# Stick-breaking scores issued for two heads at once, one on each half of TensorE's rows

## The reference, cut to what matters

```python
def stick_breaking_attention(q, k, v):
    # A[t,s] = sigmoid(z_ts) * prod_{s<j<t} (1 - sigmoid(z_tj)), s < t;  o_t = sum_s A[t,s] v_s
    ...
    def block(args):
        q_blk, start = args
        z = jnp.einsum("bhqd,bhkd->bhqk", q_blk, kh) * scale
        q_pos = start + jnp.arange(SB_BLOCK, dtype=jnp.int32)
        mask = k_pos[None, :] < q_pos[:, None]
        log_keep = jnp.where(mask, jax.nn.log_sigmoid(-z), 0.0)
        between = lax.cumsum(log_keep, axis=3, reverse=True) - log_keep
        weight = jnp.where(mask, jnp.exp(jax.nn.log_sigmoid(z) + between), 0.0)
        return jnp.einsum("bhqk,bhkd->bhqd", weight, vh)
    ...
```

## Time and profile before

| | us |
|---|---|
| median of 3 runs | 1779.08 |
| lowest, highest | 1778.29, 1780.57 |
| the profiled execution's own time | 1775.79 |
| its span, first to last instruction | 1773.9 |
| PE busy | 1720.2 |
| DVE, ACT, POOL busy | 283.3, 197.6, 143.5 |
| mean granted TensorE clock | 0.982 |

### The profile page before, as it was taken

One profiled execution on the slowest core, in us unless ns is written; L12 is line 12 of the kernel. 1 busy time (PEld: TensorE's weight loads), 2 busy tenths in 40 slices (PEclk: granted clock), 3 DMA queues, 4 the chain that ended last, 5 costly groups with the idle time before them and its releaser, 6 DMA issues.

```text
span 1773.9 us, 41158 instructions
## 1 busy us (share of the span) xinstructions
PE 1720.2 (97%) x18812; PEld 1268.8 (72%) x18812; DVE 283.3 (16%) x553; ACT 197.6 (11%) x462; POOL 143.5 (8%) x164
## 2 busy tenths in 40 slices
PE   7999999999999995999999999999999999999997
PEld 6788577777778755777777776777776777777774
DVE  2333310000434334001001001001001001001002
ACT  3123220000322323000000000000000000000000
POOL 2233200000123322000000000000000000000000
PEclk9999999999999996999999999999999999999999
DMA  8213244443320324999999999899899899899892
GB/s 308 73 46 120 95 152 168 168 153 132 122 102 27 119 95 143 308 350 341 315 350 333 322 351 326 296 349 353 304 350 346 278 348 352 303 352 354 298 353 97
DMA packets 311445, 432.58 MB, mean 244 GB/s; under 512 B 9051, under 2 KB 263261, under 8 KB 311277
## 3 DMA queue, kind: packets, MB, share of 16 engines
q1 hardware_dynamic: 310396, 427.75, 69.9%
q0 software_dynamic: 672, 2.14, 0.4%
q10 hardware_dynamic: 208, 0.08, 0.0%
HBM read 428.90 MB, written 1.05 MB: 242 GB/s over the span
## 4 chain that ended last, share of the span: by engine, by line
PE 94%; DVE 2%; ACT 1%; issue 1%; POOL 1%; SPq 0%; DMA 0%; DVEq 0%
PE ps L848 34%; PE ps L861 23%; PE ps L751 8%; PE ps L488 7%; PE ps L762 3%; PE ps L629 3%; PE ps L497 3%; PE ps L873 2%; PE ps L600 1%; PE ps L615 1%; PE ps L826 1%; PE ps L611 1%; PE ps L621 1%; PE ps L512 1%; PE ps L519 1%
## 5 line engine op out<-in xcount | busy, mean ns | idle before, releaser
L848 PEld LDWEIGHTS ps<-bv_sb,ring 128*64 128x64 f32 x14336 | 598.1, 137 | 92.6 <-issue 92.6
L848 PE MATMUL ps<-bv_sb,ring 128*64 128x96 f32 x14336 | 619.0, 247 | 6.2 <-issue 5.6
L861 PE MATMUL ps<-ring,LT_sb 128*96 128x512 f32 x896 | 410.9, 601 | 0.0
L861 PEld LDWEIGHTS ps<-ring,LT_sb 128*96 128x96 f32 x896 | 137.0, 163 | 191.6 <-issue 179.3
L1505 DVE TENSOR_TENSOR LT_sb<-LT_sb,ps 128x192 f32<-128x192 f32 x112 | 39.7, 354 | 916.8 <-ACT LT_sb L1132 916.8
L751 PE MATMUL ps<-hT_sb,ring 128*128 128x256 f32 (+1 forms) x768 | 155.7, 362 | 0.0
L751 PEld LDWEIGHTS ps<-hT_sb,ring 128*128 128x128 f32 x768 | 136.0, 190 | 24.6 <-issue 9.1
L1132 ACT ACTIVATE LT_sb<-ps 128x192 f32<-128x192 f32 x112 | 37.0, 330 | 948.9 <-PE ps L848 948.9
L488 PE MATMUL ps<-hT_sb,ring 128*128 128x256 f32 x608 | 139.4, 388 | 0.0
L488 PEld LDWEIGHTS ps<-hT_sb,ring 128*128 128x128 f32 x608 | 117.6, 196 | 17.0 <-DVE qk_sb L1220 0.5
L1556 POOL TENSOR_SCALAR small<-small 128x1 f32<-128x1 f32 x16 | 4.1, 254 | 1346.3 <-ACT XT_sb L951 1320.5
(11 more groups left out here) (259 smaller groups left out, 1002.9 us busy)
## 6 DMA issues: line engine op xcount, KB each, us to landing
ring<-in_moe_w_gate SPq DMA_DIRECT2D x112, 1024.0 KB, 5.9
ring<-in_moe_w_up SPq DMA_DIRECT2D x112, 1024.0 KB, 8.9
ring<-in_moe_w_down SPq DMA_DIRECT2D x112, 1024.0 KB, 10.8
ring<-in_ffn_w_gate SPq DMA_DIRECT2D x11, 1024.0 KB, 5.3
ring<-in_ffn_w_up SPq DMA_DIRECT2D x11, 1024.0 KB, 7.9
ring<-in_ffn_w_down SPq DMA_DIRECT2D x11, 1024.0 KB, 9.8
ring<-in_w_in SPq DMA_DIRECT2D x14, 768.0 KB, 6.4
ring<-in_w_out SPq DMA_DIRECT2D x8, 768.0 KB, 5.5
```

Source lines behind the costliest of these rows:

```text
L848: ins = mm(o[lo:lo + P // 2, :], w[:, k, i * P + lo:i * P + lo + P // 2], xgT[:, k, :], start=(k == 0), stop=(k == KD - 1))
L861: ins = mm(bank(2 + half)[0:SLOTS, :], moe_hid[c % 2][:, i, :], d[:, i, half * 512:(half + 1) * 512], start=(c == 0 and i == 0), stop=(c = ...
```

## The change: what it does

`sb_scores` takes a pair of heads `p` in place of one head. It issues the 256-column matmul of head 2p (partitions 0 to 63), that of head 2p+1 (partitions 64 to 127), then the two 128-column matmuls. The pairs stand ahead of the loop (heads 0 and 1) and at the end of levels 1, 3 and 5; at the end of levels 0, 2, 4 and 6 there are no scores any more. Each head's signal `sbz_ps` still comes from its 128-column matmul.

The two heads of a pair are in PSUM at once: even heads keep bank 6, odd heads get bank 3 (`sb_bank`), for the scores and for the running sum. Bank 3 was used by the key products and by `X M1` of group 1. So the first scores wait until VectorE has read the key products (`LT_ready`, `AT_ready`), `X M1` goes to bank `g`, the bank of the product that it follows, and the state product in bank 3 waits until the last head is through (`sb_expo`).

```diff
+        def sb_bank(h):
+            return bank(3 if h % 2 else 6)
...
-            def sb_scores(L, h):
-
-                if h:
-                    pe.wait_ge(sb_expo, SB_H * L + h)
+            def sb_scores(L, p):
+
+                if p:
+                    pe.wait_ge(sb_expo, SB_H * L + 2 * p)
                 else:
                     pe.wait_ge(*evac_sem(L, S_Z + 1))
-                pe.wait_ge(*evac_sem(L, S_SB + 1 + 2 * (h // 2)))
-                r = (h % 2) * SB_D
-                kh, qh = sk_v[r:r + SB_D, h // 2, :], sq_v[r:r + SB_D, h // 2, :]
-                o = bank(6)
-                mm(o[:, 0:T], kh[:, 0:P], qh[:, 0:T], start=True, stop=True)
-                mm(o[:, T:T + P], kh[:, P:T], qh[:, P:T], start=True, stop=True).then_inc(sbz_ps, 1)
+                    pe.wait_ge(LT_ready, 2 * (L + 1))
+                    pe.wait_ge(AT_ready, 2 * (L + 1))
+                pe.wait_ge(*evac_sem(L, S_SB + 1 + 2 * p))
+                heads = [(sk_v[r:r + SB_D, p, :], sq_v[r:r + SB_D, p, :], sb_bank(2 * p + r // SB_D)) for r in (0, SB_D)]
+                for kh, qh, o in heads:
+                    mm(o[:, 0:T], kh[:, 0:P], qh[:, 0:T], start=True, stop=True)
+                for kh, qh, o in heads:
+                    mm(o[:, T:T + P], kh[:, P:T], qh[:, P:T], start=True, stop=True).then_inc(sbz_ps, 1)
...
-                        ins = mm(bank(2 + g)[:, (pr % 4) * P:(pr % 4 + 1) * P], XT[:, pr, :], M1[:, pr, :],
+                        ins = mm(bank(g)[:, (pr % 4) * P:(pr % 4 + 1) * P], XT[:, pr, :], M1[:, pr, :],
...
-                    sb_scores(L, l + 1)
+                    if l % 2:
+                        sb_scores(L, (l + 1) // 2)
...
                 per_head(2, lambda h: qk[:, h, 0, P:T], lambda h: S[:, h, :], ks_ps)
+                pe.wait_ge(sb_expo, SB_H * (L + 1))
                 per_head(3, lambda h: qk[:, h, 1, P:T], lambda h: S[:, h, :], None)
```

More of the change, by code:

```diff
@@ L500, in project @@
                     ins.then_inc(step_sem(L, n)[0], 1)
-            def sb_scores(L, h):
-                if h:
-                    pe.wait_ge(sb_expo, SB_H * L + h)
+            def sb_scores(L, p):
+                if p:
+                    pe.wait_ge(sb_expo, SB_H * L + 2 * p)
                 else:
                     pe.wait_ge(*evac_sem(L, S_Z + 1))
-                pe.wait_ge(*evac_sem(L, S_SB + 1 + 2 * (h // 2)))
-                r = (h % 2) * SB_D
-                kh, qh = sk_v[r:r + SB_D, h // 2, :], sq_v[r:r + SB_D, h // 2, :]
-                o = bank(6)
-                mm(o[:, 0:T], kh[:, 0:P], qh[:, 0:T], start=True, stop=True)
-                mm(o[:, T:T + P], kh[:, P:T], qh[:, P:T], start=True, stop=True).then_inc(sbz_ps, 1)
+                    pe.wait_ge(LT_ready, 2 * (L + 1))
[6 more added lines that the diff above has]
+                    mm(o[:, T:T + P], kh[:, P:T], qh[:, P:T], start=True, stop=True).then_inc(sbz_ps, 1)
             def sb_cumsum(L, h):
                 pe.wait_ge(sb_keep, SB_H * L + h + 1)
-                o = bank(6)
+                o = sb_bank(h)
                 mm(o[:, 0:3 * P], tri, sp[:, h % 2, :], start=True, stop=True)
@@ L1288, in sb_mask @@
                         dve.wait_ge(sb_weight, SB_H * L + h - 1)
-                    V.scalar_tensor_tensor(zm[:, h % 2, :], bank(6)[:, 0:3 * P], SB_D ** -0.5, sbmask,
+                    V.scalar_tensor_tensor(zm[:, h % 2, :], sb_bank(h)[:, 0:3 * P], SB_D ** -0.5, sbmask,
                                            ALU.mult, ALU.mult).then_inc(sbz_ready, 1)
@@ L1302, in sb_exponent @@
                     dve.wait_ge(sbc_ps, SB_H * L + h + 1)
-                    V.tensor_tensor(zm[:, h % 2, :], zm[:, h % 2, :], bank(6)[:, 0:3 * P], ALU.subtract)\
+                    V.tensor_tensor(zm[:, h % 2, :], zm[:, h % 2, :], sb_bank(h)[:, 0:3 * P], ALU.subtract)\
                         .then_inc(sb_expo, 1)
@@ L1332, in mixer @@
                             dve.wait_ge(X_ready, 2 * (6 * L + l - 1) + g + 1)
-                            V.tensor_tensor(X[:, s, :], X[:, s, :], bank(2 + g).rearrange("p (a b) -> p a b", a=4),
+                            V.tensor_tensor(X[:, s, :], X[:, s, :], bank(g).rearrange("p (a b) -> p a b", a=4),
                                             ALU.subtract).then_inc(X_ready, 1)
```

## The result

| us | before | changed |
|---|---|---|
| median of 6 runs | 1779.60 | 1786.43 |
| lowest, highest | 1778.21, 1780.92 | 1783.01, 1788.03 |
| span of the profiled execution | 1773.9 | 1781.9 |

The ratio is 1.0036, 95% interval 1.0026 to 1.0046: 6.4 us slower, 4.6 to 8.2 (the two medians lie 6.8 us apart). The forecast was 5.8 us faster.

A forecast was written before the change was run, and what follows sets the result against it. PE, holding 94% of the chain of waits, was taken as the bound. Gains of 3.6 us in one layer (clock up) and 2.2 in the other (clock fallen) gave 1779.1 - 5.8 = 1773.3 us, range 1770.5 to 1779.0.

The forecast's parts named there:

- Rival E: Gain given back as a later stage waits for something unmoved, such as expert weights; 1778.5 us, chance 0.07.
- steps 1, 5, 6: Pairs ahead of the loop, in levels 1 and 3, in level 5: 0.22 us later each; only levels 1 and 3 lose, 0.44.
- sign of A: Main forecast (0.53), halves overlapping: second head's 256-column record starts within 0.05 us of the first head's second record.
- step 3: Level 0 loses head 1's scores and the 1.71 us wait; idles in two pieces; gain 1.97 us, 0.57 if the clock falls.
- even chance: Clock falling to half for 3.4 us around level 0: expected in one of the two layers.
- Step 4: Levels 2 and 4 have no scores: 2.10 us gained; GpSimd's keep mask keeps its 0.2 us cover.
- steps 2, 7, 8: Key-product wait free; level 6 swaps 1.05 us of scores for about 0.95 waiting on `XT`; wait for head 7's exponent free.
- B: Pair's halves run end to end, sharing only gaps; each pair 0.65 us over one head; 1776.7 us, chance 0.23.
- C: Each change of half in a pair empties the array for 0.20 us; slower, 1782 us, chance 0.09.
- D: Clock falls in more places, as at level 6's new wait, some 1.5 us a layer; 1776.3 us, chance 0.08.

The follow-up runs named there:

- bef_minus6: Kernel before, with PE's stream ahead of the expert loop 6 instructions shorter (redundant waits left out, 2 put back as satisfied waits); 1791.60 us, ratio 1.0069.
- head_by_head: Changed kernel with the expert loop in its old place, all of a pair's even-head matmuls issued ahead of the odd head's; 1770.95 us, ratio 0.9962 to before.
- one_then_other: Changed kernel, expert loop in its old place, even head's matmuls first and the odd head's waiting on a semaphore until they are done; 1777.65 us, ratio 0.9992.

## Why the prediction was wrong, point by point

- **What failed: "Later stages are chained on PE too, so the gain is passed on."** The sum counted what the removed and moved matmuls do and took an instruction that only waits for free. It missed that the 6 that went move everything behind them, the expert loop too, and that this costs 6.6 and 6.5 us of waiting and about 1 us of slower clock: 12.3 us in bef_minus6, 14.0 between the two forms of the changed kernel. Rival E looked for a late transfer of weights, at a price of 5 us, and no rival had the place of the code. The rows of before held the hint: two waits of 2.8 us put down to "issue", passed over since the change left that stage alone. With the loop's place restored, 6.3 us of the loops' 8.0 do arrive; the longer jumps take 1.5.
- **Pairs (steps 1, 5, 6): right in kind, mis-sized.** I took 1.27 us for a pair, from a picture in which the records of the program start in order. Measured is 1.05 (from 120.40 + 0.89 = 121.29, the end of the updates, to 124.12 - 1.78 = 122.34, in the way of the prediction), the cost of a single head, and head_by_head shows that the order is indifferent. The odd head's first record starts 0.007 us after the even head's first, sooner than the sign of A asked for. The lower bound, both wholly side by side, was the true one. Steps 1 and 5 had 0.22 us a pair; it is 0.
- **Level 0 (step 3): right.** Two idle pieces, 0.69 and 0.83 us where 0.7 and 1.05 were said, ended by L1617 (L1610 before); the running sum of head 1 starts 13.7 us after the first scores (the row at 116.75, and 0.1 more, since it is 0.91 long where it was 0.81 before) against 15.8, 2.1 gained for 1.97.
- **Clock: better than the forecast's even chance.** No fall in either loop of the changed kernel, nor in those of the 8 experiments that lack the 1.71 us wait; a fall in both loops of all three kernels that have it.
- **Levels 2 and 4 (step 4): 0.93 and 1.04 us for 1.05 each,** from the first update product of the level to that of the next. Step 4 had the cover of 0.2 us stay. Behind level 2 it did not: in level 3 GpSimd's keep mask waited 0.49 us for VectorE's softplus, which no longer had PE's scores as cover, and ended at 137.21, 0.06 us ahead of the running sum's row; timeline of POOL, changed kernel:

```profile
133.22 2.50 POOL L1617 TENSOR_TENSOR BM<-LT_sb,cst 128x512 f32<-128x512 f32 x2 [2.39 <-PE ps L605]
136.22 0.99 POOL L1622 TENSOR_TENSOR sbp<-sbp,cst 128x384 f32<-128x384 f32 x1 [0.49 <-DVE sbp L1305]
```

- **Level 6 and the added waits (steps 2, 7, 8): right.** 0.78 us for `XT_sb` where 0.95 was said; none on the key products or on the exponent of head 7.
- **Sum per layer: 4.0 us for 3.6 (clock up).** With the loop's place put back the change is worth 6.3 us by the medians, where the forecast had 5.8. That these lie so close is luck in part: 5.8 took one layer with the clock down, and 6.3 is 8.0 less 1.5 us of longer stalls.
- **The rivals.** B (end to end, 0.65 us more a pair than side by side) does not happen; one_then_other, which forces an order with a stop on top, is at 0.97 more. C (a turn between halves costs) is refuted: the halves don't take turns. D did not occur in the loops. The sign of C, slower, came true for a reason that it did not have. Its price at 0.30 us a turn, by its own sum, is 1784.1, not 1784.5.

## What to carry to other kernels

In this kernel PE pays at each backward jump of its loop, and how much depends on where the loop begins in pieces of 256 instructions. Loops on the other engines, and other kernels, were not tried, but the check is cheap. Before judging an edit ahead of a loop, count the instructions that it adds or takes, the pure waits included, look at the waits on "issue" at the jump in both profiles, and if they changed, add satisfied waits where the engine idles until they are back; only then compare. And the float32 score matmuls of two heads, 64 rows each on different halves, cost PE here what one head's cost (1.05 us), in either order of issue that was tried.

## What the runs showed that was not expected

- A backward jump on PE leaves it idle for 2.6 to 3.6 us when the first fetched piece holds matmuls (98 instructions from the target on were the fewest), and for 8.4 to 9.4 us when it holds the target and one instruction more. The second fetch comes 6.0 to 6.7 us after the first.
- The halves of the rows start 0.007 us apart (interleaved) or 0.013 us apart (head by head).
- 3.4 us at half clock followed each 1.71 us wait of PE in the mixer loop (6 of 6). It followed none of the shorter waits that took its place in the other nine profiles.
